# Routing in smaller steps, and a loop of fourteen turns, in a fused mixer and mixture-of-experts layer

## The reference

```python
x = x + merged @ w_o
t = rmsnorm(x, g_ffn)
logits = t @ w_router + b_router
top_v, top_i = lax.top_k(logits, TOP_K)            # 4 of 32
top_w = jax.nn.softmax(top_v, axis=-1)
for e in range(N_EXPERTS):
    gu = t @ w_gate_up[e] + b_gate_up[e]           # 1024 -> 2048
    gate = jnp.minimum(gu[:, :D_FF], 7.0)
    up = jnp.clip(gu[:, D_FF:], -7.0, 7.0)
    y = ((up + 1.0) * gate * jax.nn.sigmoid(1.702 * gate)) @ w_down[e] + b_down[e]
    out = out + combine[:, e:e + 1] * y
return rmsnorm(x + out, g_final)
```

## Time and profile before

| | |
|---|---|
| median of three runs | 1176.23 us |
| the profiled execution's own time | 1175.9 us |
| its span | 1174.1 us |
| TensorE busy | 1149.0 us (98%) |
| VectorE, ScalarE, GpSimd busy | 336.7, 268.2, 23.4 us |
| moved by DMA | 452.12 MB, mean 385 GB/s |
| granted clock of TensorE, mean | 0.995 |

### The profile page before, as it was taken

One profiled execution on the slowest core, in us unless ns is written; L12 is line 12 of the kernel. 1 busy time (PEld: TensorE's weight loads), 2 busy tenths in 40 slices (PEclk: granted clock), 3 DMA queues, 4 the chain that ended last, 5 costly groups with the idle time before them and its releaser, 6 DMA issues.

```text
span 1174.1 us, 14477 instructions
## 1 busy us (share of the span) xinstructions
PE 1149.0 (98%) x6269; PEld 580.4 (49%) x6269; DVE 336.7 (29%) x658; ACT 268.2 (23%) x449; POOL 23.4 (2%) x37
## 2 busy tenths in 40 slices
PE   9999999999999999999999999999999999999987
PEld 9998999985333333333343324333333333333322
DVE  6678997663211010101121102111010101010102
ACT  7767776342100100000011001110010001010002
POOL 1000112000000000000000000000000000000000
PEclk9999999999999999999999999999999999999999
DMA  9769766789999999999999999999999999999996
GB/s 298 211 221 306 243 217 218 278 328 351 429 432 431 431 430 429 431 430 419 433 431 431 430 429 431 430 429 435 431 430 432 429 429 433 429 426 428 428 424 276
DMA packets 69228, 452.12 MB, mean 385 GB/s; under 512 B 6874, under 2 KB 42178, under 8 KB 48580
## 3 DMA queue, kind: packets, MB, share of 16 engines
q1 hardware_dynamic: 68912, 451.27, 94.0%
q10 hardware_dynamic: 276, 0.30, 0.1%
HBM read 450.49 MB, written 1.07 MB: 385 GB/s over the span
## 4 chain that ended last, share of the span: by engine, by line
PE 83%; DMA 16%; another core or an unknown queue 0%; DVE 0%; ACT 0%; issue 0%; POOL 0%; POOLq 0%; DVEq 0%; ACTq 0%
PE pj L1632 31%; PE pj L1372 15%; PE gb L1671 14%; DMA quad<-in_w_gate_up 8%; DMA pair<-in_w_gate_up 4%; DMA slot<-in_w_down 3%; PE s L1678 2%; PE pj L1607 2%; PE gb L1600 2%; PE pt L1678 2%; PE ga L1600 2%; PE pj L1644 1%; PE pj L1355 1%; PE pj L1381 1%; PE pt L1381 1%; PE ga L1671 1%
## 5 line engine op out<-in xcount | busy, mean ns | idle before, releaser
L1632 PE MATMUL pj<-quad,GL 128*64 128x512 f32 x1664 | 367.5, 599 | 8.4 <-DMA quad<-in_w_gate_up 8.1
L1632 PEld LDWEIGHTS pj<-quad,GL 128*64 128x64 f32 x1664 | 117.4, 138 | 255.3 <-issue 239.3
L1203 DVE TENSOR_SCALAR x_sb<-pj 128x512 f32<-128x512 f32 x32 | 22.1, 691 | 704.0 <-PE pj L1632 704.0
L1671 PE MATMUL gb<-quad,x_sb 128*64 128x512 f32 x832 | 184.3, 595 | 0.0
L752 ACT ACTIVATE pj<-x_sb 128x512 f32<-128x512 f32 x31 | 18.6, 602 | 476.1 <-DVE x_sb L1203 476.1
L1372 PE MATMUL pj<-hT_hi,w_hi 128*128 128x256 f32 x424 | 120.7, 285 | 0.0
L1372 PE MATMUL pj<-hT_hi,w_lo 128*128 128x256 f32 x424 | 119.8, 283 | 0.0
L1671 PEld LDWEIGHTS gb<-quad,x_sb 128*64 128x64 f32 x832 | 57.4, 137 | 124.6 <-issue 124.6
L1372 PE MATMUL pj<-hT_lo,w_hi 128*128 128x256 f32 x424 | 117.9, 278 | 0.0
L889 DVE TENSOR_TENSOR w_lo<-mix,w_hi 128x1024 fp32r<-128x1024 f32 x79 | 95.4, 1248 | 38.1 <-ACT w_hi L578 37.2
L578 ACT ACTIVATE w_hi<-mix 128x2048 fp32r<-128x2048 f32 x38 | 72.7, 1913 | 49.7 <-PE pj L1372 42.8
(11 more groups left out here) (373 smaller groups left out, 1019.6 us busy)
## 6 DMA issues: line engine op xcount, KB each, us to landing
quad<-in_w_gate_up SPq DMA_DIRECT2D x48, 4096.0 KB
quad<-in_w_down SPq DMA_DIRECT2D x24, 4096.0 KB
pair<-in_w_gate_up SPq DMA_DIRECT2D x16, 2048.0 KB, 49.9
mix<-in_w_in SPq DMA_DIRECT2D x27, 1024.0 KB, 5.7
slot<-in_w_gate_up SPq DMA_DIRECT2D x16, 1024.0 KB, 7.5
slot<-in_w_down SPq DMA_DIRECT2D x11, 1024.0 KB, 33.6
quad<-in_w_gate_up SPq DMA_DIRECT2D x8, 1024.0 KB
quad<-in_w_gate_up SPq DMA_DIRECT2D x4, 2048.0 KB
```

Of the source, the lines that this page charges most:

```text
L1203: v.tensor_scalar(gate, pj[0][:, :], LIMIT, None, ALU.min).then_inc(gate_ready, 1)
L1632: last = mm(pj[q // 2][h:h + SLOTS, :], hg[:, c, i, :], w[:, q * 512:(q + 1) * 512], start=(first and c == 0), stop=(c == GU_CHUNKS - 1), ...
L1671: last = mm(to[h:h + SLOTS, :], actT[:, f % 4, f // 4, :], w[:, a * D + q * 512:a * D + (q + 1) * 512], start=(f == 0), stop=(f == KT - 1))
```

## The change

Five edits, all in the order and the grain of the same work:

1. The second tile's last sum is made in two halves of 256 elements (`add_last_half`), each counted in `x2_last`; its square is made in halves too (`square_half`), and the transposes of c = 2 wait for the first half alone.
2. On VectorE `rms_inverse(1)`, `logits(1)` and `mask(1)` come ahead of `positions(0)` and `select(0, 0)`; on TensorE the tile-1 router products come ahead of the position products.
3. The gather's order becomes (0, 0), (1, 0), (0, 1), (1, 1), (2, 0), then (3, 0) ahead of chunk 2 of expert 0, and (2, 1), (3, 1) ahead of chunk 3 as before.
4. The bias of expert 0 moves from ahead of chunk 2 to ahead of chunk 7.
5. The loop has fourteen turns and takes in pair 14; the part behind it goes. The loads in twos of that pair signal on the places' own semaphores by 4 and by 1, and there is a new wait at the third chunk of each quad.

```diff
-LOOPED = range(1, 14)
+LOOPED = range(1, 15)
...
-    if _h in IN_TURNS:
+    if _h >= QUAD_TO and _h in IN_TURNS:
+        SIGNAL.append((_p, 4 if _p in QUAD_AT else 1))
+    elif _h in IN_TURNS:
         SIGNAL.append((QUAD_AT[(_h - IN_TURNS[0]) // 4 % len(QUAD_AT)], _n))
...
+            def square_half(half):
+                act.wait_ge(sumsq2, 3 + half)
+                act.activation(squares[:, half * CC:(half + 1) * CC].rearrange("p (i n) -> p i n", i=2),
+                               strips(1, 1)[:, 2 * half:2 * half + 2, :], ACT.Square,
+                               accum_out=stat[:, 53 + half:54 + half]).then_inc(sumsq2, 1)
...
             for t in range(TT):
                 act.wait_ge(x2_last, t + 1)
-                square(1, t)
+                if t == 0:
+                    square(1, t)
+                else:
+                    square_half(0)
                 act.wait_ge(h2T_psum, 3 + 2 * t)
                 act.activation(h2T_mid[:, :, t * P:(t + 1) * P], ...
+                if t == 1:
+                    act.wait_ge(x2_last, 3)
+                    square_half(1)
...
+            def add_last_half(half):
+                two = slice(2 * half, 2 * half + 2)
+                v.tensor_tensor(strips(1, 1)[:, two, :],
+                                x_sb[:, 1, 512:].rearrange("q (n i) -> q i n", i=4)[:, two, :],
+                                out_banks[1][1][:, :].rearrange("q (n i) -> q i n", i=4)[:, two, :], ALU.add).then_inc(x2_last, 1)
...
             dve.wait_ge(chunk_done, MIX_CHUNKS)
-            add_last(1)
+            add_last_half(0)
+            add_last_half(1)
             mask(0)
...
-            positions(0)
-            select(0, 0).then_inc(sel_first, 1)
             rms_inverse(1)
             logits(1)
             mask(1)
+            positions(0)
+            select(0, 0).then_inc(sel_first, 1)
...
-                    pe.wait_ge(x2_last, tiles[0] + 1)
+                    pe.wait_ge(x2_last, 1 + tiles[0] * (c - 1))
...
             x2_transpose(3, (1,))
+            pe.wait_ge(h2T_ready, 4)
+            route(2, 1)
+            pe.wait_ge(h2T_last, 2)
+            route(3, 1).then_inc(router_psum, 1)
             pe.wait_ge(prefix_ready, 2)
             pe.wait_ge(mask_ready, 1)
             mm(pos_at[0], tri, msk[:, 0, :], start=True, stop=True).then_inc(pos_psum, 1)
             mm(pos_at[1], ones, msk[:, 0, :], start=True, stop=False)
-            pe.wait_ge(h2T_ready, 4)
-            route(2, 1)
-            pe.wait_ge(h2T_last, 2)
-            route(3, 1).then_inc(router_psum, 1)
...
+                    if first and c == 2:
+                        gather_tile(3, 0)
...
-                    if first and c == 2:
+                    if first and c == GU_CHUNKS - 1:
                         pe.wait_ge(late_loaded, 64)
                         pe.wait_ge(onehot_ready, 1)
                         gate_up_bias(0, start=False)
...
+            pe.wait_ge(mask_ready, 2)
+            mm(pos_at[1], tri, msk[:, 1, :], start=False, stop=True).then_inc(pos_psum, 1)
             pe.wait_ge(sel_first, 1)
             gather_tile(0, 0)
-            gather_tile(2, 0)
-            pe.wait_ge(mask_ready, 2)
-            mm(pos_at[1], tri, msk[:, 1, :], start=False, stop=True).then_inc(pos_psum, 1)
             gather_tile(1, 0)
-            gather_tile(3, 0)
             pe.wait_ge(sel_ready, 1)
             gather_tile(0, 1)
             gather_tile(1, 1)
+            gather_tile(2, 0)
...
                 if h % 4 == 0:
                     pe.wait_ge(loaded[place], p * 64 + 16 * (units - 4 * LOOPED[0]))
+                if h % 4 == 2:
+                    pe.wait_ge(loaded[place + 2], 16 * (COUNT[LOAD_OF[QUAD_TO + i * EXP_CHUNKS + c]] - 1) + p // LOOPED[-1] * 16)
...
-            for n in range(2 * LOOPED[-1] + 2, N_EXP - 2):
...
-                down(i, chunk_at)
```

More of the change, by code:

```diff
@@ L1103, in sum_squares @@
             def sum_squares(t):
-                dve.wait_ge(sumsq2, TT + t + 1)
-                v.tensor_reduce(stat[:, 20 + t:21 + t], stat[:, 48 + 4 * t:50 + 4 * t], AX.X, ALU.add).then_inc(sumsq2_ready, 1)
+                dve.wait_ge(sumsq2, TT + 2 * t + 1)
+                v.tensor_reduce(stat[:, 20 + t:21 + t], stat[:, 48 + 4 * t:50 + 5 * t], AX.X, ALU.add).then_inc(sumsq2_ready, 1)
             def rms_inverse(t):
@@ L1776, in chunk_in_turn @@
                     assert PLACE[2 * at_p + i, c] == h + turn and PLACE_OF[h + turn] == place + h % 4
-                    assert SIGNAL[LOAD_OF[last + turn]][0] == place and COUNT[LOAD_OF[last + turn]] == units + 4 * (at_p - LOOPED[0])
+                    if h + turn < QUAD_TO:
+                        assert SIGNAL[LOAD_OF[last + turn]][0] == place and COUNT[LOAD_OF[last + turn]] == units + 4 * (at_p - LOOPED[0])
                 if h % 4 == 0:
                     pe.wait_ge(loaded[place], p * 64 + 16 * (units - 4 * LOOPED[0]))
+                if h % 4 == 2:
+                    pe.wait_ge(loaded[place + 2], 16 * (COUNT[LOAD_OF[QUAD_TO + i * EXP_CHUNKS + c]] - 1) + p // LOOPED[-1] * 16)
                 return quads[place][:, bass.ts(h % 4, CHUNK)]
```

## The result

The changed kernel takes **1179.41 us** in the median (7 runs, 1178.53 to 1181.09), before it was 1176.23 (7 runs). The ratio of the two is 1.0029, 95% interval 1.0020 to 1.0038: slower by 0.29%, 3.4 us (3.2 by the medians). The profiled execution took 1181.09 us, its span is 1178.9. The forecast was no change, with a range up to 1178.0.

What follows compares the result with a forecast made beforehand. The weight stream was taken as the bound; +0.17 us for its start and -0.2 for earlier chunks summed to 0.0, loop and end 0, so no change: 1176.2 us median, range 1173.6 to 1178.0.

Steps and rivals of the forecast that it cites:

- Bound and place: Whole run: the weight stream sets the end; the change acts at 270 to 290 us, prize at most 4.9 us.
- Halves: Second tile's last sum: each half takes 0.5 us, logits(1) starts 0.2 us earlier; bounds 0.3 gain to 0.35 loss.
- VectorE's order: Logits ahead of the other half's positions on VectorE: the 0.2 us gain is given back, sel_ready 0.1 us later.
- The step that failed first: Routing on PE: position products moved behind the router product cost nothing; gather tiles take 0.55 us; chunk 0 0.3 us later.
- The step that failed second: Weight stream: chunk 8, 0.85 us later, is covered by 2.5 us of loads still queued.
- Rival (b): The queue runs dry later: chunk 8 and the next four come late, 0.5 to 1 us lost, 1177.0; chance 0.10.
- the ideal queue: Weight stream at 2.44 us a chunk: its start moves from 277.1 to 277.27, +0.17 us, set by chunk 0.
- First bias: Expert 0's bias moved ahead of chunk 7: chunks 2 to 6 come 0.2 us earlier, counting -0.2 us in the stream.
- rival (a): The stream's ramp in 278 to 290 us fills as the bias moves: 1 to 3.5 us faster, 1174.0; chance 0.18.
- Loop: Fourteen turns with new waits in each: 0 us, no stall from one more turn.
- rival (c): PE becomes the bound through 84 new loop waits: +14 us at 0.3 us each, 1190; chance 0.06.

Runs made afterwards that it cites:

- e11: Kernel before with eight idle products at full clock between expert 0's gate and up (behind chunk 7) and the gather ahead of expert 1; ratio 1.0016.
- e8: Kernel before with eight idle products at full clock between the gather and the first weights' product, ahead of chunk 0; ratio 1.0009.
- e5: Kernel before with only the last sum and last square made in halves; 1176.07 us, ratio 0.9999.
- e3: Changed kernel with five idle products filling TensorE's two gaps in the routing, four in the first and one in the second; 1177.33 us, ratio 1.0007.
- e7: Changed kernel with four idle products in the first of TensorE's two routing gaps alone; 1177.22 us, ratio 1.0008.
- e6: Kernel before with the new order of the gather alone; ratio 1.0006.
- e2: Changed kernel with the loop put back to thirteen turns, so the routing edits alone; 1179.00 us, ratio 1.0020.
- e4: Kernel before with only expert 0's bias moved ahead of chunk 7; 1175.91 us, ratio 0.9998.
- e1: Kernel before with the loop of fourteen turns alone; 1176.08 us, ratio 0.9998.

## Why the prediction was wrong

**Bound and place: right.** The end is the weight stream's, and the change acts through when chunks come back between 270 and 300 us. e11 shows it, and e8 at the edge of its interval: idle products there, with PE at full clock and with 14.8 us (e11) and 10.9 us (e8) of waits for weights left over the whole span, lengthen the run.

**Halves: the cost right, the gain by luck.** A half takes 0.57 us (0.5 forecast). `logits(1)` starts 271.73 - 268.11 = 3.62 us behind the mixer, before 271.28 - 267.46 = 3.82: the 0.2 of the forecast. But it was put down to the halves, and e5 with the halves alone has 3.79. There the position products still stand ahead of `route(2, 1)`; the 0.2 came only with edit 2, which moves them behind it. The Trainium skill's rule on 16-byte lines ("SBUF — State Buffer", Door 1: The DMA port swizzle) would make these reads slower than contiguous ones, and 0.57 against 0.42 for 256 elements is consistent with it; that the price is not 1.05 but 0.57 is the run's.

**VectorE's order: right in size, wrong in what it leaves open.** Timeline of DVE after, against the earlier trace rows:

```profile
272.55 0.19 DVE L1139 TENSOR_TENSOR msk<-rep,lg 128x32 f32<-128x32 f32 x1
272.65 0.18 DVE L1147 SCALAR_TENSOR_TENSOR GL<-ga,msk 128x32 f32<-128x32 f32 x1
272.87 0.54 DVE L1179 TENSOR_SCALAR GL<-iota,GL,stat 128x64 f32<-128x64 f32 x2
...
273.66 0.54 DVE L1179 TENSOR_SCALAR GL<-iota,GL,stat 128x64 f32<-128x64 f32 x2
```

The second selection starts 5.55 us behind the mixer, before 5.62: 0.07 earlier, forecast 0.1 later.

**The step that failed first** is the one that says "On PE the two position products move behind the router product: 0.3 us in PE's idle time, cost nothing", and with it the gather's tiles at 0.55 us each. The prediction looked at PE's idle time as room. The early gather tiles and the position products had been what kept PE busy there; with `select(0, 0)` behind the second mask no tile is ready to stand in the wait, PE is idle for 0.73 us, and the clock falls to the lower level. That is 1.63 us on chunk 0 (9.41 against 7.78 in e3) and on all that PE does behind it, chunk 8 with it (31.66 against 30.03), on top of the 0.24 on chunk 0 that the order costs by itself. The forecast for chunk 0 was +0.3, measured was +1.87. In no rival does the clock appear.

**The step that failed second** is "Chunk 8, 0.85 us later, is covered by what is still queued". Rival (b) named it and gave it a chance of 0.10. e11 shows it: with chunks 0 to 7 in time and chunk 8 1.78 us late, onto a cover of 2.5, the run is 1.9 us longer. The cover was worked out as if the stream kept its full rate down to the last byte queued, and in e11 the rate fell with 0.4 MB left. D8 is +1.03 in e3 and e7 and +0.86 in e6, and they are 0.7 to 0.9 us over before, but each of their intervals reaches down to no change, so that 0.85 us alone costs anything is likely and not shown. (One reading is slightly off: chunk 3's issue stands at 284.58 in the trace of before, not at 284.4. By the ideal queue the start then does not move at all, instead of by 0.17 us.)

**How the loss divides is not shown.** In the changed kernel chunk 0 was 1.87 us late and chunk 8 2.66. No run has chunk 0 late and chunk 8 in time. e2's windows put the shortfall at chunk 0, after the queue ran empty (8 GB/s from 279 to 280 us); that e11, with chunk 0 in time, lost no less than e8, with both late, speaks for chunk 8.

**First bias: wrong sum, no effect.** Chunks 2 to 6 were to count -0.2 us in the stream. Their being 1.06 us earlier in e4 was worth nothing that can be measured, and the rate in 278 to 290 did not rise (352 GB/s against 357). So rival (a), 1 to 3.5 us, falls but for its smallest part, which e4's interval would still hold.

**Loop: right.** e1 is at 0.9998, and rival (c) falls. The 64 records of an expert's gate and up in the loop take 13.95 us after as before. The Trainium skill's rule on taken branches ("Runtime: NRT & Kernel Launch", Instruction fetch mechanics) could have added a stall by one more turn; in e1 PE goes from expert 27's `down` to the bias of expert 28, the first of the new turn, at 1052.26 without idle time, and the time shows no stall either.

**Not settled:** the shape of idle time that drops the clock (0.23, 0.73, then 0.26 did, in two kernels; 0.60, then 0.40 did not, in one execution); whether edit 2 drops it without edit 3, since no run has edit 2 alone; and whether the loss is 2.4 us (e2) or 3.4 (the changed kernel against its own runs of before), since the intervals overlap.

## What to carry to other kernels

Useful work that stands in TensorE's waits can do two things: it gets done, and it keeps the clock up. Before moving it out, ask what the gap that it leaves does to the products behind it; some idle products into a free bank are the cheap test. And where a stream of loads sets the time, the bytes queued over the full rate say too much about how late a release may come: here 1 MB queued looked like 2.5 us of cover, and a release 1.8 us late cost about 1.9 us.

## What the runs showed of the hardware

- The granted clock fell to 0.50 after a gap of 0.73 us and one of 0.26, with 0.4 us of a small product between them and a wait of 0.23 us some 2 us earlier, in a kernel in which PE had been busy nearly all along; it stayed there for about 3.4 us (changed kernel, and e2 alike). With gaps of 0.60 and 0.40 (e6), or 0.23 and 0.27 (e7), it stayed at 1.00.
- A gather tile (four records of 128x128) takes 0.85 us from start to start at the lower clock and 0.44 to 0.55 at the full one.
- When an issue came with an estimated 0.4 MB still queued (e11), the 16 DMA engines moved 334 GB/s over the next 8.5 us, at a share of 0.98; with about 1 MB queued (before) it was 423 at 1.01. A share near 1 does not say that the rate is full.
- With nothing queued (changed kernel) the stream fell to 4 GB/s, and it was back at 319 GB/s 1.5 to 2.5 us behind the next issue at 279.50.
